# The last weight chunk of sixteen experts in four column transfers, the running sum carried into PSUM, the output in four stores

## The reference

```python
def expert_choice_ffn(h, w_router, w_gate, w_up, w_down):
    """h: (B,S,D). Each sequence is its own routed set; each expert picks its top-C tokens."""
    b, s, d = h.shape
    cap = CAPACITY_FACTOR * s // N_EXPERTS                       # 32 tokens of each expert
    aff = jax.nn.softmax((h @ w_router).astype(jnp.float32), axis=-1)
    gates, idx = lax.top_k(jnp.swapaxes(aff, 1, 2), cap)
    xs = jax.vmap(lambda hb, ib: hb[ib])(h, idx)
    hid = jax.nn.silu(jnp.einsum('becd,edf->becf', xs, w_gate)) * jnp.einsum('becd,edf->becf', xs, w_up)
    out = jnp.einsum('becf,efd->becd', hid, w_down) * gates[..., None].astype(h.dtype)
    return jax.vmap(lambda ob, ib: jnp.zeros((s, d), h.dtype).at[ib.reshape(-1)].add(ob.reshape(-1, d)))(out, idx)

# at the end of the second block
h2 = modulate(rms_norm_2(x, norm_pre_ffn[l]), shift2, scale2)
y = expert_choice_ffn(h2, w_router[l], w_gate[l], w_up[l], w_down[l])
x = x + gate2[:, None, :] * rms_norm_2(y, norm_post_ffn[l])
```

## Time and profile before

| | us |
|---|---|
| median of 3 runs | 2382.78 |
| lowest and highest of them | 2379.72, 2384.42 |
| the profiled execution: its own time | 2379.06 |
| the profiled execution: its span | 2377.3 |
| TensorE busy | 1824.5 |
| VectorE busy | 808.5 |
| ScalarE busy | 531.3 |

### The profile page before, as it was taken

How to read it: one execution, slowest core, us unless ns; L and a number is a source line. 1 busy time by engine, 2 the same in 40 slices (tenths; PEclk the granted TensorE clock), 3 DMA queues, 4 the chain that set the end, 5 groups by cost and what they waited for, 6 DMA issues and landing times.

```text
span 2377.3 us, 28602 instructions
## 1 busy us (share of the span) xinstructions
PE 1824.5 (77%) x12548; PEld 1178.4 (50%) x12548; DVE 808.5 (34%) x1229; ACT 531.3 (22%) x800; POOL 90.8 (4%) x140
## 2 busy tenths in 40 slices
PE   7998999999988998977666566666656665566665
PEld 6888889988888997864121111122111121111121
DVE  4655667656556777653010101001100110010002
ACT  5634533355454434441000000000000000000000
POOL 1200000012000000010000000000000000000000
PEclk9999999999999999977877788788877877877777
DMA  7345467754454776347999999999999999999996
GB/s 241 107 135 194 142 213 238 240 163 134 142 165 154 249 246 204 125 188 323 429 429 430 429 429 429 429 429 430 429 429 429 430 430 428 428 430 429 428 429 265
DMA packets 171067, 739.78 MB, mean 311 GB/s; under 512 B 6672, under 2 KB 133136, under 8 KB 146240
## 3 DMA queue, kind: packets, MB, share of 16 engines
q1 hardware_dynamic: 168592, 731.27, 77.3%
q0 software_dynamic: 2352, 6.69, 0.8%
HBM read 736.88 MB, written 1.05 MB: 310 GB/s over the span
## 4 chain that ended last, share of the span: by engine, by line
DMA 49%; PE 41%; DVE 5%; ACT 2%; issue 2%; POOL 1%; SPq 0%; POOLq 0%; DVEq 0%; ACTq 0%
PE PS L325 39%; DMA WB<-in_w_down 24%; DMA WB<-in_w_up 23%; DVE WL L1493 1%; ACT WH L974 1%; DVE X L1488 1%; DMA W<-in_w_gate 1%; POOL T L2234 1%; DVE C L1488 1%; DMA S<-in_post_mix_g 1%; PE PS L398 0%; DMA W<-in_w_in 0%; PE PS L422 0%; DVE S L1557 0%; DVE S L1488 0%
## 5 line engine op out<-in xcount | busy, mean ns | idle before, releaser
L325 PE MATMUL PS<-WB,XS 128*32 128x352 f32 x3072 | 363.5, 635 | 211.3 <-DMA WB<-in_w_up 124.2
L325 PE MATMUL PS<-WB,S 128*32 128x512 f32 x1408 | 268.8, 759 | 156.5 <-DMA WB<-in_w_down 78.8
L1493 DVE TENSOR_TENSOR WL<-W,WH 128x2048 fp32r<-128x2048 f32 x141 | 322.9, 2290 | 146.1 <-ACT WH L974 146.0
L325 PEld LDWEIGHTS PS<-WB,XS 128*32 128x32 f32 x3072 | 115.6, 141 | 456.6 <-issue 177.9
L1488 DVE SCALAR_TENSOR_TENSOR S<-S,PS 128x352 f32<-128x352 f32 (+1 forms) x110 | 63.3, 587 | 784.8 <-ACT S L1458 751.2
L325 PE MATMUL PS<-HTh,WH 128*128 128x256 f32 x1064 | 310.5, 292 | 18.8 <-DVE HTl L1488 8.4
L974 ACT ACTIVATE WH<-W 128x2048 fp32r<-128x2048 f32 x141 | 268.8, 1908 | 199.7 <-PE PS L325 186.7
L325 PE MATMUL PS<-HTl,WH 128*128 128x256 f32 x1064 | 305.0, 287 | 0.0
L325 PE MATMUL PS<-HTh,WL 128*128 128x256 f32 x1064 | 304.9, 287 | 0.0
L325 PEld LDWEIGHTS PS<-WB,S 128*32 128x32 f32 x1408 | 72.1, 127 | 342.2 <-issue 222.2
L325 PEld LDWEIGHTS PS<-HTh,WH 128*128 128x128 f32 x1064 | 208.3, 196 | 21.8 <-DVE WL L1493 10.4
(11 more groups left out here) (269 smaller groups left out, 2105.3 us busy)
## 6 DMA issues: line engine op xcount, KB each, us to landing
WB<-in_w_down SPq DMA_DIRECT2D x64, 2816.0 KB, 36.0
WB<-in_w_gate SPq DMA_DIRECT2D x48, 2816.0 KB, 35.9
WB<-in_w_up SPq DMA_DIRECT2D x48, 2816.0 KB, 35.9
C<-in_w_gate SPq DMA_DIRECT2D x16, 2816.0 KB, 36.2
C<-in_w_up SPq DMA_DIRECT2D x16, 2816.0 KB, 37.2
W<-in_w_in SPq DMA_DIRECT2D x31, 1024.0 KB, 5.4
S<-in_w_ada SPq DMA_DIRECT2D x24, 1024.0 KB, 5.4
W<-in_w_gate SPq DMA_DIRECT2D x22, 1024.0 KB, 7.8
```

The lines of the kernel that those rows point to most:

```text
L325: return e.matmul(o, l, r, start=start, stop=stop, skip_group_check=True)
L1493: e.tensor_tensor(M.WL[i][:, :], M.W[:, 2048 * (m % NW):2048 * (m % NW) + 2048], M.WH[i][:, :].bitcast(F32), ALU.subtract).then_inc(*up("l ...
```

## The change

Four things change, all for the last expert (ex = 15):

- its last chunk of `w_down` is loaded by four transfers of 3, 3, 3 and 2 slots instead of one, each with a semaphore of its own, and the matmuls run in the order of the slots, waiting for one piece at a time (`down_last`);
- between the third chunk's matmuls and these, four matmuls with the identity matrix put the running sum `YA` of the other 15 experts into banks 0 to 3 (`carry`), and the last scatter accumulates on it (`scatter_last`, in the order t, then hf), so VectorE's four last adds go;
- the norm reads banks 0 to 3 instead of `YA`;
- the output is stored in four parts of 128 x 512.

```diff
+PIECES = ((0, 1, 2), (3, 4, 5), (6, 7, 8), (9, 10))
...
+    def carry(ex):
+
+        e.wait_ge(*at("hidden", ex, 1))
+        for t in range(2):
+            for hf in range(2):
+                e.wait_ge(*free("scat", ex - 1, hf, t))
+                mm(PS[:, 2 * t + hf, :], M.ID, M.YA[:, t, 512 * hf:512 * hf + 512], True, False)
+
+    def scatter_last(ex):
+        e.wait_ge(*free("sg", ex))
+        for t in range(2):
+            for hf in range(2):
+                if t == 0:
+                    e.wait_ge(*at(f"dn{hf}", ex))
+                mm(PS[:, 2 * t + hf, :], M.SG[ex % 2][:, 128 * t:128 * t + 128], M.DN[ex % 2][:, hf, :], False, True).then_inc(
+                    *up("yfull", "moe", t, hf))
+
+    def down_last(ex):
+
+        b = M.BIG[C.loads % len(M.BIG)]
+        C.loads += 1
+        v, hh = b.rearrange("p (s d) -> p s d", d=512), M.HH[ex % 2]
+        for j, piece in enumerate(PIECES):
+            e.wait_ge(*at(f"piece{j}", 0))
+            for s in piece:
+                u, hf = (33 + s) // 2, (33 + s) % 2
+                g = 32 * (u % 4)
+                ins = mm(PS[g:g + 32, 4 + hf, :], hh[:, u, :], v[:, s, :], False, u >= 18)
+                if s == 9:
+                    ins.then_inc(*up("down4", ex, 0))
+        taken(ins)
+        same(("down4", ex, 1), ("chunk", C.loads - 1))
...
-        for i in range(4):
+        for i in range(3 if ex == 15 else 4):
             down(ex, i)
-        for hf in range(2):
+        if ex == 15:
+            carry(ex)
+            down_last(ex)
+            scatter_last(ex)
+        for hf in range(0 if ex == 15 else 2):
             scatter(ex, hf)
...
-    post_squares(("moe",), M.YA)
+    post_squares(("moe",))
...
-            for t in range(2):
+            for t in range(2 if ex < 15 else 0):
...
-    post_norm(("moe",), M.GA[:, 1, :], M.YA, M.YA)
+    post_norm(("moe",), M.GA[:, 1, :], tmp=M.YA)
...
+                if (ex, wname, i) == (15, "w_down_2", 3):
+                    for j, piece in enumerate(PIECES):
+                        lo, hi = 512 * piece[0], 512 * piece[-1] + 512
+                        e.dma_start(buf[:, lo:hi], w[:, BIG * i + lo:BIG * i + hi]).then_inc(*up(f"piece{j}", 0, by=16))
+                    continue
...
-        e.dma_start(out[0, 128 * t:128 * t + 128, :], M.X[:, t, :]).then_inc(*up("out", t, by=16))
-    e.wait_ge(*at("out", 1))
+            e.dma_start(out[0, 128 * t:128 * t + 128, 512 * h:512 * h + 512], M.X[:, t, 512 * h:512 * h + 512]).then_inc(
+                *up("out", t, h, by=16))
+    e.wait_ge(*at("out", 1, 1))
```

More of the change, by code:

```diff
@@ L893, in scatter @@
         for t in range(2):
-            ps = spare(("scat", ex, hf, t)) if ex < 15 else PS[:, 2 * hf + t, :]
+            ps = spare(("scat", ex, hf, t))
             mm(ps, M.SG[ex % 2][:, 128 * t:128 * t + 128], M.DN[ex % 2][:, hf, :], True, True).then_inc(
                 *up("full", "scat", ex, hf, t))
+    def carry(ex):
[26 more added lines that the diff above has]
+        same(("down4", ex, 1), ("chunk", C.loads - 1))
     def down(ex, i):
@@ L2210, in vector_program @@
                 e.tensor_copy(M.DN[e2][:, 1, :], PS[:, 5, :]).then_inc(*up("dn1", ex))
-            for t in range(2):
+            for t in range(2 if ex < 15 else 0):
                 o = M.YA[:, t, 512 * hf:512 * hf + 512]
                 e.wait_ge(*at("full", "scat", ex, hf, t))
[L2214 to L2218, removed]
+                i, _ = C.banks.uses[("scat", ex, hf, t)]
+                ps, done_ = PS[:, 4 + i, :], freed("scat", ex, hf, t)
                 if ex == 0:
@@ L2223, in vector_program @@
                     e.tensor_tensor(o, o, ps, ALU.add).then_inc(*done_)
-                if ex == 15:
-                    same(("yfull", "moe", t, hf), ("ya", t, hf))
     e.wait_ge(*at("ga_moe"))
-    post_norm(("moe",), M.GA[:, 1, :], M.YA, M.YA)
+    post_norm(("moe",), M.GA[:, 1, :], tmp=M.YA)
 def gpsimd_program(e, C):
```

## The result

The changed kernel takes 2376.24 us (median of 10 runs, 2374.28 to 2378.74) against 2381.8 us before (10 runs, 2377.98 to 2384.42). The ratio is 0.9978, with a 95% interval of 0.9970 to 0.9987: 5.2 us faster, between 3 and 7. Forecast were 2378.7 us and 4.1 us, with 0.62 on a difference within 0.2% and 0.34 on more. The middle of the ratio lies just beyond 0.2%, and the interval spans that bound.

The account below looks back on a forecast made before the run. The expert stage is bound by weight DMA (share 1.00, 429 GB/s), so only the tail can change. Norm chain 3.5 + store 0.6 = 4.1 us, from the 2382.78 us median to 2378.7; range 2374.5 to 2382.8.

Parts of the forecast that it names:

- Only the tail can change: Expert stage lasts as long as its weights arrive; only the 19.1 us behind the last transfer's landing can change.
- Split transfer: Last chunk in four pieces: lands 0.2 us later, at 2358.4, hidden behind the carry; early arrival not used.
- Carry: Four fp32 matmuls on TensorE before the last chunk's: about 3.5 us, covered by 3.08 idle, overrunning by 0.35.
- Four rounds, not six: Last chunk's 11 matmuls in slot order: four rounds by column group, 3.55 us to the scatter's start, not six (5.1).
- Rival 1: Last chunk's matmuls go strictly in turn, six rounds: +1.7 us, gain 2.4, 2380.4 us; chance 0.22.
- Copies, scatter and squares: After the last matmuls: bank 4's copy hidden, bank 5's unblocked, four adds gone, squares read PSUM; first mean square at 2364.9.
- From there the old chain holds: Norm, from tile 0's mean square to last scaling: unchanged 5.76 us, ending 2370.66 against 2374.15, 3.5 us earlier.
- Stores: Output's last store is 256 KB instead of 512: landing 0.6 us shorter, bounds 0 to 0.64.
- Rivals 2 and 3: Last chunk's pieces each pay a 1.3 us gap, gain 2.35 (chance 0.06); half clock over the carry, slower (0.05).
- Rival 4: No carry overrun, no filling (0.45), or measurement adds: over 4.8 us faster, 2377.5; upper part of the forecast's 0.67.
- Rival 3: TensorE at half clock over the carry: carry 7.0 us late, 2385.7 us, or 2391.8 if low through the scatter; chance 0.05.

Follow-up runs that it names:

- pieces of 3, 3, 4, 1: Changed kernel with carry one chunk earlier, pieces of 3, 3, 4, 1 slots, last scatters by half, then token tile: 2374.96 us, ratio to before 0.9973.
- own groups: Changed kernel with carry one chunk earlier, pieces of 3, 4, 3, 1 slots, each slot's column group next after its predecessor's: 2372.5 us, ratio to before 0.9963.

## Why the prediction was right, step by step

- *Only the tail can change.* Right: in 1200 us of the expert stage the DMA share is 1.00 at 429 GB/s after too. The prediction allowed for the spread of the runs, but not for where it lies: the part before L varies by 6.5 us from profile to profile.
- *Split transfer, 0.2 us later, hidden, its early arrival unused.* Right: 0.22 us, and the run with one transfer has the same tail.
- *Carry, 3.5 us, overruns by 0.35.* The block took 3.63 us (2357.94 to 2361.57), 0.1 more, for a reason that no run shows. The overrun was 0.47 us, counted from where one transfer would have let the last chunk start (L + 6.71 + 0.05, 2361.10).
- *Four rounds, not six.* Right: 3.56 us from the block's start to the scatter's. The loads of the block (8, 4, 4, 2, 2, 1, 1) show all four groups busy in the first two rounds, which takes looking past two waiting matmuls; the matmuls themselves start in fours too, four within 0.04 us at each half pass of these rounds. Rival 1 is out. So is, for the starts of these column tiles, the rule of the Trainium skill that matmuls start in program order, which the prediction quotes ("TensorE: Matmul & The Clock Gate", "Part 3: Packing small matmuls — row/col tiling"): this case's trace does not agree with it. For the completion events the order holds: the runs with pieces of 3, 3, 4, 1 and with own groups bear it out.
- *Copies, scatter and squares.* Scatter to first mean square 2.74 us, forecast 2.75.
- *"From there the old chain holds".* This is the step that was wrong, in the gain's favour. Mean square to the last scaling took 3.58 us instead of 4.35, because the power was faster by 0.38 us for each of two token tiles, 0.76 together. Reading PSUM was priced at its own instruction's time alone, not by what it frees for GpSimd, although earlier norms in the same trace show it. With this term the sum is 4.1 + 0.76 = 4.9 us, and 0.12 less for the overrun (0.47 instead of 0.35): 4.7, measured 4.77.
- *Stores, 0.6 us.* Right: 0.62.
- *Rivals 2 and 3.* The pieces came 1.9 us apart and 1.25 for the last, with no gap of 1.3 us, and the clock was at its upper level through the carry in all nine profiles that have one. Neither occurred.
- *Rival 4, over 4.8 us.* The medians show it (5.2 us by the ratio), but not for its reasons: the carry did overrun and its passes did need filling. The power and the spread of the runs made it.

Rival 3 was not far off, though. In the run without a carry (split transfer) the clock was at 0.50 from the third landing, 2354.01, for 3.3 us:

```profile
2354.00:2357.30 3.30, 3.25 (x16) 0.77 (x18) 0.00 (x0) 0.00 (x0) 0.00 (x0) 0.50 0.51 209
```

There TensorE caught up before the last piece. What such a stretch would cost in front of a carry, no run shows.

The forecast time of 2378.7 us is 2.5 us above the measured 2376.24. Of that, 1.0 is the median of before, which is lower over ten runs (2381.8) than over three (2382.78); 0.7 is the tail (4.77 instead of 4.1); and 0.8 is what the medians differ by beyond the tails (5.6 against 4.77), which fits the spread of the runs. The chances put 0.62 on a change within 0.2%, and the median came out just beyond. The range took in the missing 0.76 us because it was 8 us wide, not because the sum had it. With the missing term known, 4.9 us against a bound of 4.8, the two cases would have been even.

## What to carry to other kernels

Work that fills idle time is free only if the engine can catch up before the wait that counts. The same four matmuls cost 2 us behind the third chunk. One chunk earlier they cost nothing, although the idle stretch there (2.3 us) was shorter than they are, because another idle stretch followed before the last transfer. Two remedies for the same wait do not add (1.53 and 2.46 us alone, 2.48 together), so price the second one with the first in place. When an operand moves from SBUF to PSUM, look at which other engine was running beside the instruction, not only at the instruction's own time.

## What the hardware showed that was not expected

- GpSimd's 128x1 power takes 0.56 us beside a VectorE product with one PSUM and one SBUF input, and 0.94 us beside the same product with both inputs in SBUF.
- Matmuls on different column groups start ahead of a matmul in front of them that waits for its own group, past two such (8, 4, 4, 2, 2, 1, 1 loads). Their semaphore events were seen in program order: in the run with pieces of 3, 3, 4, 1 the event of a matmul that was over at 2359.3 came at 2360.2.
- Twelve profiles differ by up to 6.5 us ahead of the changed place, with the same work there (third landing 2350.95 to 2357.49).
